# A hybrid encoder step: score products of two attention maps, issued in turn in two row halves of TensorE

## What is computed

```
q2 = q.reshape(B, H, Q, 2, DK_A)                 # DK_A = 64
k2 = k.reshape(B, H, K, 2, DK_A)
s = einsum('bhqmd,bhkmd->mbhqk', q2, k2) * (DK_A ** -0.5)
s = s + t5_bias(qpos, kpos, table)[None, None]   # one bias for both maps
s = where(kpos // 64 <= qpos // 64, s, NEG)
p = softmax(s, axis=-1)
a = p[0] - lam * p[1]
o = einsum('bhqk,bhkd->bhqd', a, v)              # then rmsnorm and w_o
```

## Time and profile before

| | |
|---|---|
| time, median of 3 runs | 3769.35 us (3768.32 to 3771.99) |
| span of the profiled execution | 3763.8 us, 5.55 us below that median |
| PE busy | 3405.2 us (90%) |
| DVE busy | 2365.6 us (63%) |
| ACT busy | 1097.7 us (29%) |
| POOL busy | 931.3 us (25%) |
| mean granted clock of TensorE | 0.928 of full speed |
| PE's share of the chain that ended last | 68%, then DVE 16% |

### The profile page before, as it was taken

One profiled execution on the slowest core, in us unless ns is written; L12 is line 12 of the kernel. 1 busy time (PEld: TensorE's weight loads), 2 busy tenths in 40 slices (PEclk: granted clock), 3 DMA queues, 4 the chain that ended last, 5 costly groups with the idle time before them and its releaser, 6 DMA issues.

```text
span 3763.8 us, 53583 instructions
## 1 busy us (share of the span) xinstructions
PE 3405.2 (90%) x19257; PEld 3177.4 (84%) x19257; DVE 2365.6 (63%) x3742; ACT 1097.7 (29%) x2465; POOL 931.3 (25%) x419
## 2 busy tenths in 40 slices
PE   7989999899899999999898687878799999999997
PEld 5878888788699999999897577777689999999997
DVE  6554555645765566556767766666676665566675
ACT  3331323323411111111322555464631111111142
POOL 1102110021133333333332001101033333333331
PEclk8878898888899999999999898989999999999998
DMA  3111101111011111111111110101011111111111
GB/s 112 31 31 41 36 25 36 31 41 36 12 46 40 45 43 43 42 44 45 47 40 47 31 25 18 31 7 31 6 31 43 46 40 46 40 45 40 57 35 59
DMA packets 227327, 145.32 MB, mean 39 GB/s; under 512 B 34852, under 2 KB 208372, under 8 KB 226964
## 3 DMA queue, kind: packets, MB, share of 16 engines
q1 hardware_dynamic: 164792, 107.34, 9.7%
q10 hardware_dynamic: 62300, 34.62, 3.2%
HBM read 124.51 MB, written 17.42 MB: 38 GB/s over the span
## 4 chain that ended last, share of the span: by engine, by line
PE 68%; DVE 16%; issue 9%; ACT 5%; DMA 1%; DVEq 0%; ACTq 0%
PE ps L441 20%; PE ps L443 19%; PE ps L442 19%; PE ps L529 2%; DVE t L1316 2%; DVE t L1373 2%; PE ps L555 2%; DVE t L1306 2%; DVE t L1280 2%; PE ps L577 2%; PE ps L639 1%; DVE t L1366 1%; ACT t L948 1%; ACT t L942 1%; DVE t L1290 1%
## 5 line engine op out<-in xcount | busy, mean ns | idle before, releaser
L441 PE MATMUL ps<-t,t 128*128 128x384 f32 (+3 forms) x5144 | 1758.9, 342 | 113.4 <-DVE t L1280 45.9
L443 PE MATMUL ps<-t,t 128*128 128x384 f32 (+3 forms) x5144 | 1717.2, 334 | 0.0
L442 PE MATMUL ps<-t,t 128*128 128x384 f32 (+3 forms) x5144 | 1716.1, 334 | 0.0
L441 PEld LDWEIGHTS ps<-t,t 128*128 128x128 f32 (+1 forms) x5144 | 988.5, 192 | 194.4 <-DVE t L1280 52.4
L422 POOL TENSOR_TENSOR t<-t,t 128x1024 fp32r<-128x1024 f32 x205 | 405.4, 1977 | 2758.1 <-PE ps L443 2740.7
L443 PEld LDWEIGHTS ps<-t,t 128*128 128x128 f32 (+1 forms) x5144 | 992.0, 193 | 7.7
L442 PEld LDWEIGHTS ps<-t,t 128*128 128x128 f32 (+1 forms) x5144 | 993.0, 193 | 3.1
L424 POOL TENSOR_TENSOR t<-t,t 128x1024 fp32r<-128x1024 f32 x205 | 525.4, 2563 | 16.1
L1280 DVE TENSOR_TENSOR t<-t,ps 128x384 f32<-128x384 f32 x720 | 365.0, 527 | 250.1 <-PE ps L443 248.9
L1114 ACT ACTIVATE t<-ps 128x384 f32<-128x384 f32 x176 | 86.6, 493 | 1037.2 <-PE ps L443 1037.2
L1576 DVE TENSOR_SCALAR t<-t 128x2 f32 (+1 forms) x88 | 56.1, 637 | 423.1 <-ACT t L1126 423.1
(11 more groups left out here) (146 smaller groups left out, 2965.3 us busy)
## 6 DMA issues: line engine op xcount, KB each, us to landing
t<-in_w_ffn_in SPq DMA_DIRECT2D x88, 512.0 KB, 3.8
t<-in_w_ffn_out SPq DMA_DIRECT2D x44, 512.0 KB, 3.7
t<-in_w_qkv_a SPq DMA_DIRECT2D x24, 512.0 KB, 3.8
out<-t ACTq DMA_DIRECT2D x24, 512.0 KB, 3.3
t<-in_w_ple_gate SPq DMA_DIRECT2D x16, 512.0 KB, 3.9
t<-in_x_prompt ACTq DMA_DIRECT2D x8, 512.0 KB, 7.7
t<-in_w_o_a SPq DMA_DIRECT2D x8, 512.0 KB, 4.0
t<-in_w_q_b SPq DMA_DIRECT2D x8, 512.0 KB, 3.8
```

The lines of the kernel that those rows point to most:

```text
L441: pe.matmul(out, a_hi, b_hi, start=start, stop=False, skip_group_check=True)
L442: pe.matmul(out, a_hi, b_lo, start=False, stop=False, skip_group_check=True)
L443: return pe.matmul(out, a_lo, b_hi, start=False, stop=stop, skip_group_check=True)
```

## The change

`scores_a` takes both maps of a tile. For each piece it issues the same three products, but each of them for map 0 in rows 0 to 63 and at once for map 1 in rows 64 to 127. The bias products of map 0 follow behind the products of all pieces, then those of map 1. `s_done` is raised after each map's bias as before. There is one wait, at the start, for the exponential of map 1 of the tile before. In the loop of `attention_a` the call for map 1, which stood behind the turn of the output, is gone.

```
-            def scores_a(t, m, uc):
-                e = 2 * t + m
-                if e >= 2:
-                    pe.wait_ge(exp_done, uc["s"](e - 1))
+            def scores_a(t, uc):
+                if t:
+                    pe.wait_ge(exp_done, uc["s"](2 * t))
                 a, b = columns(t)
...
                 for c0, c1, kh, kl, kc in pieces:
                     n = c1 - c0
-                    three(psf[:, s0 + c0:s0 + c1], q_hi[lo:hi, a:b], q_lo[lo:hi, a:b], kh[lo:hi, kc:kc + n],
-                          kl[lo:hi, kc:kc + n], True, False)
...
+                    for q, k, start in ((q_hi, kh, True), (q_hi, kl, False), (q_lo, kh, False)):
+                        for m in range(2):
+                            lo, hi = 64 * m, 64 * m + 64
+                            pe.matmul(psf[:, 1024 * m + c0:1024 * m + c1], q[lo:hi, a:b], k[lo:hi, kc:kc + n],
+                                      start=start, stop=False, skip_group_check=True)
+                first = max(0, width - (256 if t < 8 else 192))
+                for m in range(2):
+                    for c0, c1, _, _, _ in pieces:
+                        b0, b1 = max(c0, first), c1
+                        if b0 < b1:
+                            o = 256 - width
+                            for part in (bias_hi, bias_lo):
+                                last = pe.matmul(psf[:, 1024 * m + b0:1024 * m + b1], ident_r[:, :], part[:, b0 + o:b1 + o],
+                                                 start=False, stop=part is bias_lo, skip_group_check=True)
+                    last.then_inc(s_done, 1)
...
                     if t <= 8:
-                        scores_a(t, 0, uc)
+                        scores_a(t, uc)
...
-                    if t <= 8:
-                        scores_a(t, 1, uc)
```

More of the change, by code:

```diff
@@ L530, in transposes @@
                 m.then_inc(t_done, 1)
-            def scores_a(t, m, uc):
-                e = 2 * t + m
-                if e >= 2:
-                    pe.wait_ge(exp_done, uc["s"](e - 1))
+            def scores_a(t, uc):
+                if t:
+                    pe.wait_ge(exp_done, uc["s"](2 * t))
                 a, b = columns(t)
-                lo, hi = 64 * m, 64 * m + 64
-                s0 = 1024 * m
+                width = 128 * (t + 1) if t < 8 else PAST + TS
                 if t < 8:
-                    pieces = [(c, min(c + 512, 128 * (t + 1)), k_hi, k_lo, c) for c in range(0, 128 * (t + 1), 512)]
+                    pieces = [(c, min(c + 512, width), k_hi, k_lo, c) for c in range(0, width, 512)]
                 else:
```

## The result

The changed kernel takes 3866.35 us (median of 4 runs, 3861.15 to 3870.62), the kernel before, run beside it, 3770.67 us (3768.32 to 3772.87). The ratio is 1.0257, with a 95% interval from 1.0239 to 1.0275: slower. The forecast was 3878 us, in a range from 3785 to 3931.

What follows compares the result with a forecast made beforehand. Within a head PE was seen running on while DVE waits; the new wait closes a serial ring. Heads of 66.5 us, eight making 532 against 428.2, add 104, plus 5 behind them: 3873 profiled, 3878 us median, range 3785 to 3931.

Steps and rivals of the forecast that it cites:

- The ring: Layer 0 attention: scores, maximum, DVE work, second maximum, exponential, next scores run without overlap; S + Q for t=1 to 8.
- The start of t=1: In each head, t=1 waits for the second exponential and starts 4.37 us into the head (4.02 before).
- S: From first score product to map 0's bias end, pairs running at once: 23.6 us a head at low clock, 14.7 high.
- The middle value: A score pair costs at least 512 columns if its weight loads don't overlap: 3.2 us a head more; not adopted.
- Q: Rest of a round, from map 0's bias end to the next scores: 36.9 us a head, 5.97 for t=6.
- What becomes late: At the low clock, ACT waits for transposes and value products now behind both maps: 3.8 us a head.
- Clock: In each head, t=1 to 4 run at the low level, and t=5 to 8 three parts in four.
- The tail: After a head's last tile, the next projection may begin at low clock: 0 to 15 us in four heads, 5 taken.
- The high level all through: Rival, chance 0.07: pairs count as full work and the clock never falls; a head 56.0 us, +20, total 3789.
- No pairing: Rival, chance 0.13: score products still run one after the other and the wait remains; 82.0 us a head, total 4002.
- Faster: Rival, chance 0.04: high clock, and pairing also hides 0.66 us of switching and latency per S; 50.7 a head, 3747.
- The emptying of PSUM: From the skill: emptying PSUM may become the bound; by it the gain in PE time is worth nothing.

Runs made afterwards that it cites:

- the run with the filled wait: Changed kernel with 16 throwaway products of 128 rows and 256 columns in PE's wait of each tile: 3793.61 us, ratio 1.0063 to the kernel before.
- the first run: Changed kernel with all of map 0's score products listed before map 1's, same wait and place: 3905.42 us, ratio 1.0351 to the kernel before.

## Why the prediction was right

- **The ring.** Right, and its count exact: 64 waits, each ending 0.05 us or so after the read of map 1's exponential. The start of t=1 was put 4.37 us into the head; the third head begins at 360.76 and its t=1 at 365.13.
- **S, with the pairs at once.** Right. S for t=6 was put at 3.33; from the first product to the maximum it is 400.85 - 397.50 = 3.35, of which 0.04 are DVE's start. Part 3 of "TensorE: Matmul & The Clock Gate" in the Trainium skill says that products in different row groups run concurrently; this case's trace agrees, with 2.54 us for twelve products where six took that before. The middle value, a price for weight loads, was not paid. For t=4 S was put at 3.71 and took 3.22.
- **Q.** Right: put at 5.97 for t=6, measured 406.67 - 400.81 = 5.86.
- **What becomes late.** The mechanism is there, spread otherwise: DVE's low parts wait 0.70, 0.41, 0, 0.36 and 2.10 us in t=4 to 8 of the third head, 3.57 together, where 0.5, 0.25, 0.25, 1.0 and 1.8 made 3.8. In t=2 and 3, where nothing was put, they wait 0.18 and 0.34 us.
- **Clock.** Nearly right, in part by luck. Tiles 1 to 4 take 23.82 us (365.13 to 388.95) at 0.50, as 13.42 of Q with 9.86 and 0.5 had it: 23.78. That they agree so closely is luck: S is half a microsecond shorter in t=4, and the low parts' waits of t=2 to 4 are 0.7 us longer. Tiles 5 to 8 take 37.31 (to 426.26) in this head, 1.0 less than put: t=7 takes 9.82 (406.67 to 416.49) where the terms make 10.75, and 0.4 more in t=5 and 0.4 less in t=8 cancel. The windows view of these four tiles (columns as above):

```profile
388.95:397.50 8.55, 5.44 (x28) 4.70 (x28) 4.69 (x10) 3.35 (x10) 0.00 (x0) 0.70 0.01 2
397.50:406.67 9.17, 5.16 (x30) 4.21 (x31) 5.29 (x11) 3.73 (x11) 0.00 (x0) 0.83 0.00 0
406.67:416.49 9.82, 5.83 (x33) 4.75 (x34) 5.82 (x11) 4.05 (x11) 0.00 (x0) 0.83 0.00 0
416.49:426.26 9.77, 8.64 (x49) 7.83 (x49) 5.25 (x11) 3.58 (x11) 0.00 (x0) 0.65 0.01 2
```

By these clocks about half of that time was at the low level, where three parts in four were put; in t=6 the score products lay in it all the same (2.54 us). The argument that lone 64-row products kept the clock low goes further than its row: from 380 to 388 us of the kernel before such products, among others, ran at 1.00. The profile's eight heads take 528.5 us in all, 66.1 each, where 66.5 and 532 were forecast.
- **The tail: mis-sized.** "After the last tile the next head's projection may begin at the low level", for which I took 5 us. The heads grew by 528.5 - 429.9 = 98.6 and the span by 96.6, so there was no such loss but 2 us the other way. In the four heads with a projection behind them the clock right after the last tile was 1.00 (426.26 to 440 us in the third). (The 428.2 of the text for the eight heads before, from two of them, stands against 429.9 by adding up all eight.) These terms, 3.5 for the heads, 1.7 for the old heads and 7 for the tail, make up the difference of 12 us between the forecast span of 3873 and 3860.4.
- **Rivals.** The high level all through didn't come by itself; the run with the filled wait nearly made it (0.91 to 0.94 in each head), and its head of 57.2 us bears out the 56.0. No pairing was worked out at 4002, and the run that takes the pairing away took 4014, though not by a longer S as I had it: there the transposes' lateness is what grows, so that the two numbers agree is luck. Faster needed a shorter ring, and S was not the part to shorten: Q was.
- **The emptying of PSUM.** The Trainium skill, "TensorEngine Tiling (Array Packing)", PSUM Bottleneck, says that the emptying of PSUM may become the bound; that the gain in PE time is then worth nothing was my own step. As far as this change goes the ring, made of that emptying, does set the time. But my step went too far: taken away under the same wait, the pairing costs 148 us, and with the emptying put first the paired kernel is 4.3% faster than the unpaired one.

What is shown: the joint wait closes a ring, and the place ahead of the transposes costs on its own; pairing is real and gives back less than the two take; holding the clock up takes back three quarters of the loss; and DVE's order decides whether pairing pays. What stays open: what sets the level of the clock, and why the high level comes back earlier in some heads than in others.

## What to carry to other kernels

When two score maps are computed side by side, their banks come free together: follow the ring from scores to maximum to exponential to the next scores, and put its readers ahead of all other work on their queues, or the time won on TensorE is spent waiting. The transposes and value products that stood between the two maps also come later, and whoever waits for them has to be counted. And a stop of TensorE can be paid twice, once as a wait and once as clock: here throwaway products in the wait gave back 73 us.

## What was not expected of the hardware

- Products in the two row halves overlap even when they are not neighbours in the list, and one of them may start before another that stands ahead of it: in tile 4 of the first run the seventh of the list at 392.398, the fourth at 392.818. The Trainium skill, "TensorE: Matmul & The Clock Gate", Part 3, has products start strictly in the order of the list; here the measurement differs.
- The busier PE had the lower clock: with the same order on DVE and ACT it was busy for 837 of 937 us at a mean of 0.76 unpaired, and for 781 at 0.89 paired. No run here shows why.
